# Six modulations computed two at a time, and their two gates spread through DRAM

## The reference, cut to what matters

```python
def adaln(cvec, w, b):                       # w: 1024 x 6144, b: 6144
    m = jax.nn.silu(cvec) @ w + b
    return m.reshape(cvec.shape[0], N_MOD, D_MODEL)

def modulate(h, m, i):
    return h * (1.0 + m[:, i + 1][:, None, :]) + m[:, i][:, None, :]

h = modulate(rmsnorm(x, norm1_g), m, 0)      # m[0], m[1]
x = x + m[:, 2][:, None, :] * mixer(h)       # m[2], a gate
h = modulate(rmsnorm(x, norm2_g), m, 3)      # m[3], m[4]
x = x + m[:, 5][:, None, :] * moe(h)         # m[5], a gate
```

## Time and profile before

| | |
|---|---|
| timed executions | 899.17, 900.0, 901.62 us |
| profiled execution, own time | 896.39 us |
| its span, first to last instruction | 894.5 us |
| TensorE busy | 855.6 us (96%) |
| VectorE busy | 491.5 us (55%) |
| ScalarE busy | 242.8 us (27%) |
| GpSimd busy | 87.0 us (10%) |
| read from HBM | 279.82 MB |

### The profile page before, as it was taken

The page is one execution under the profiler, slowest core; times in us unless marked ns, Lnnn a source line. Parts: engine busy times, 40 slices in busy tenths (PEclk is TensorE's granted clock), DMA queues, the critical chain, the costliest instruction groups (busy, mean ns, idle before and its releaser), DMA issues.

```text
span 894.5 us, 13521 instructions
## 1 busy us (share of the span) xinstructions
PE 855.6 (96%) x4887; PEld 501.8 (56%) x4887; DVE 491.5 (55%) x1016; ACT 242.8 (27%) x398; POOL 87.0 (10%) x202
## 2 busy tenths in 40 slices
PE   3799999999999999999999999999999999999993
PEld 2387875899999874434444444444444444444441
DVE  1663384486667456245646464646464646464575
ACT  3537643444423241221111111121112121112122
POOL 8410000000001060000000000000000000000000
PEclk9999999999999999999999999999999999999997
DMA  9974877622225377499999999999999999999931
GB/s 353 343 288 163 299 290 255 141 95 95 95 95 170 149 296 317 190 413 409 416 420 403 410 420 419 404 416 419 420 421 414 420 421 421 417 420 404 421 126 70
DMA packets 76596, 280.82 MB, mean 314 GB/s; under 512 B 14340, under 2 KB 30784, under 8 KB 51584
## 3 DMA queue, kind: packets, MB, share of 16 engines
q1 hardware_dynamic: 61488, 260.06, 73.3%
q0 software_dynamic: 6352, 15.52, 4.6%
q10 hardware_dynamic: 8704, 4.54, 2.0%
HBM read 279.82 MB, written 5.51 MB: 319 GB/s over the span
## 4 chain that ended last, share of the span: by engine, by line
PE 90%; DMA 5%; DVE 3%; issue 1%; ACT 0%; ACTq 0%; DVEq 0%
PE bank L1488 26%; PE bank L1507 13%; PE bank L1516 11%; PE bank L1090 8%; PE bank L1092 7%; PE bank L1091 7%; PE bank L1476 4%; DMA chunk_raw<-in_w_ada_dram 3%; PE bank L1360 2%; DMA b_t<-in_b_ada_dram 2%; PE bank L1600 2%; PE bank L1118 1%; PE bank L1170 1%; PE bank L1404 1%; PE bank L1203 1%; PE bank L1277 1%
## 5 line engine op out<-in xcount | busy, mean ns | idle before, releaser
L1488 PE MATMUL bank<-gu,x_t 128*32 128x512 f32 (+2 forms) x1408 | 240.6, 594 | 0.0
L1488 PEld LDWEIGHTS bank<-gu,x_t 128*32 128x32 f32 (+2 forms) x1408 | 75.6, 124 | 147.4 <-issue 146.7
L2125 DVE TENSOR_TENSOR ffn_acc<-ffn_acc,bank 128x512 f32<-128x512 f32 x192 | 120.4, 683 | 7.8 <-PE bank L1516 6.6
L1507 PE MATMUL bank<-dn,a_t 128*32 128x512 f32 (+2 forms) x704 | 123.9, 596 | 0.0
L1050 ACT ACTIVATE silu_sb<-bank 128x256 f32<-128x256 f32 x34 | 13.0, 384 | 320.8 <-PE bank L1488 320.8
L2067 DVE TENSOR_TENSOR act_sb<-silu_sb,bank 128x256 f32<-128x256 f32 x34 | 14.3, 421 | 149.9 <-ACT silu_sb L1050 149.9
L1090 PE MATMUL bank<-h_hi,chunk_lo 128*128 128x384 f32 x240 | 84.2, 351 | 0.0
L2117 DVE SCALAR_TENSOR_TENSOR y_lo<-bank,slot_gate,y_hi 128x512 fp32r<-128x512 f32 x68 | 50.9, 748 | 55.8 <-ACT y_hi L1040 55.5
L1092 PE MATMUL bank<-h_hi,chunk_hi 128*128 128x384 f32 x240 | 80.6, 336 | 0.0
L1091 PE MATMUL bank<-h_lo,chunk_hi 128*128 128x384 f32 x240 | 80.4, 335 | 0.0
L747 POOL DMA_INDIRECT xg<-h_dram,slot_tok x34 | 33.9, 997 | 456.5 <-DVE slot_tok L1941 456.2
(11 more groups left out here) (359 smaller groups left out, 1043.2 us busy)
## 6 DMA issues: line engine op xcount, KB each, us to landing
gu<-in_w_gate_e_dram SPq DMA_DIRECT2D x64, 1024.0 KB, 10.3
gu<-in_w_up_e_dram SPq DMA_DIRECT2D x64, 1024.0 KB, 13.6
dn<-in_w_down_e_dram SPq DMA_DIRECT2D x64, 1024.0 KB, 14.2
chunk_raw<-in_w_ada_dram SPq DMA_DIRECT2D x24, 1024.0 KB, 8.5
chunk_raw<-in_w_in_dram SPq DMA_DIRECT2D x18, 1024.0 KB, 5.5
chunk_raw<-in_w_out_dram SPq DMA_DIRECT2D x4, 1024.0 KB, 5.1
chunk_raw<-in_w_pa_dram SPq DMA_DIRECT2D x2, 1024.0 KB, 5.0
chunk_raw<-in_w_pb_dram SPq DMA_DIRECT2D x2, 1024.0 KB, 5.0
```

The lines of the kernel that those rows point to most:

```text
L1488: mm = pe.matmul(bank[2 + u % 2][at_x, :].rearrange("p (g n) -> p g n", g=2), x_t[:, cols], wide[:, :, k, :], start=(k == 0), stop=(k == K ...
L1507: mm = pe.matmul(outs[half][at_x, :], a_t[:, cols], dn[slot_of(x, first)][:, wc], start=(k == 0), stop=(k == 1))
L2125: dve.tensor_tensor(ffn_acc[t][:, cols], ffn_acc[t][:, cols], out[:, :], ALU.add).then_inc(S["place_out"], 1)
```

## The change

- `w_ada` is now read one `k` slice a chunk, for two modulations at once: (0, 1), (3, 4) and (2, 5), eight chunks a pair. The four column groups hold two modulations by two halves, and the eight chunks accumulate in one bank. No partial sums are left over.
- For the pairs (0, 1) and (3, 4) the half is not a run of 512 columns, but columns `n * 8 + k` for four values of `k`: the moving operand is read with a stride of 8 elements. Then four plain 128-column transposes turn the bank, and VectorE needs one addition (with the bias) per modulation.
- The pair (2, 5), both gates, uses bank 7 with plain runs. VectorE adds the bias (`bias_rows`, loaded earlier) and halves the rows of gate 2, and the attention's first scores wait for it. POOL stores the rows to DRAM (`gate_dram`) and loads them back to all partitions, `gate_mix` at once and `gate_ffn` when the projections are over. `pick`, `m_late` and the eight spreading matmuls with their copies are gone.
- The first projection waits for `h_t` piece by piece, at first for one piece of ScalarE and two of VectorE.

```diff
-                if kind == "ada" and i < 8:
...
+                if kind == "ada":
+                    m, k = MODS[2 * (i // KD):2 * (i // KD) + 2], i % KD
+                    sp.dma_start(dst[:, :].rearrange("p (m n) -> p m n", m=2),
+                                 w_ada[0].rearrange("(p k) (m n) -> p k m n", k=KD, n=D)[:, k, m[0]:m[1] + 1:m[1] - m[0], :]).then_inc(loaded, 16)
...
-            pool.tensor_copy(m_late[:, :], m_row[1][:, :]).then_inc(S["late_row"], 1)
+            pool.wait_ge(S["ada_row"], NMOD)
+            for c in range(2):
+                pool.dma_start(gate_dram[c:c + 1, :].rearrange("a (q n) -> (a q) n", q=NQ), gate_rows[c:P:QW, :]).then_inc(S["gate_stored"], 16)
+            pool.wait_ge(S["gate_stored"], 32)
+            pool.wait_ge(S["gates_mm"], 16)
+
+            def spread_rows(dst, n, loaded):
+                pool.dma_start(dst[:, :, :], gate_dram[:, D * n:D * n + D].unsqueeze(0).to_broadcast([P, 2, D])).then_inc(loaded, 16)
+
+            spread_rows(gate_mix, 0, S["mix_loaded"])
             pool.wait_ge(S["w_mm"], NPROJ)
+            spread_rows(gate_ffn, 1, S["ffn_gate_loaded"])
...
-            spread_copy(0, gate_mix, 0.5)
...
+            def modulate(i):
+
+                n, (m, k) = number[("ada", i)], divmod(i, KD)
+                pe.wait_ge(chunk_loaded[slot[n]], arrival[n])
...
+                for q in range(NQ):
+                    cols = chunk_raw[slot[n]][:, q // 2 * D:q // 2 * D + D]
+                    if m < 2:
+                        mm = pe.matmul(bank[6][q * QW:(q + 1) * QW, :].rearrange("p (k n) -> p k n", k=4), cond_t[:, k, :],
+                                       cols.rearrange("p (n k) -> p k n", k=KD)[:, 4 * (q % 2):4 * (q % 2) + 4, :],
+                                       start=(k == 0), stop=(k == KD - 1))
+                    else:
+                        mm = pe.matmul(bank[7][q * QW:(q + 1) * QW, :], cond_t[:, k, :],
+                                       cols[:, 512 * (q % 2):512 * (q % 2) + 512], start=(k == 0), stop=(k == KD - 1))
+                mm.then_inc(S["ada_mm"], 1)
+
+            def turn_rows(m):
+                pe.wait_ge(S["ada_row"], m + 1)
+                for j in range(4):
+                    mm = pe.transpose(bank[6][:, j * P:(j + 1) * P], m_row[m][:, j * P:(j + 1) * P], ident[:, :])
                 mm.then_inc(S["m_spread"], 1)
...
-                        if n == 0 and k % 4 == 0:
-                            pe.wait_ge(S["h_ctx"], k // 4 + 1)
-                            pe.wait_ge(S["h_made"], k // 4 + 1)
+                        if n == 0:
+                            pe.wait_ge(S["h_ctx"], k + 1)
+                            pe.wait_ge(S["h_made"], max(k + 1, 2))
...
-                spread(n, bank[4 + n % 2], m_row[0])
-            pe.wait_ge(S["ada_row"], NADA // 2)
+            later(7)
+            pe.wait_ge(S["ada_row"], NMOD)
...
+            def modulations(m):
+
+                dve.wait_ge(S["m_spread"], m + 1)
+                by_half = bank[6][:, :].rearrange("p (j a h c) -> p a h j c", j=4, a=2, h=2)
+                for a in range(2):
+                    i = MODS[2 * m + a]
+                    dve.tensor_tensor(mod_t[:, i, :, :].rearrange("p (h j) c -> p h j c", h=2), by_half[:, a, :, :, 0:2],
+                                      b_t[:, i, :].rearrange("p (h j) -> p h j", h=2).unsqueeze(3).to_broadcast([P, 2, 4, 2]),
+                                      ALU.add).then_inc(S["mod_copied"], 1)
+
+            def gates_in_rows():
+                dve.wait_ge(S["ada_mm"], NADA)
+                dve.wait_ge(S["row_biased"], 64)
+                go(dve.tensor_tensor(gate_rows[:, :], bank[7][:, :], bias_rows[:, :], ALU.add))
+                dve.tensor_scalar(gate_rows[0:HALF, :], gate_rows[0:HALF, :], 0.5, None, ALU.mult).then_inc(S["ada_row"], 1)
```

More of the change, by code:

```diff
@@ L189, in hybrid_step @@
         ob_hi = at("ob_hi", [P, CT, NTOK], EX + 111.25, F32R)
-        m_late = at("m_late", [P, D], 28)
-        m_row = [at(f"m_row{i}", [P, D], EX + 155.5 + 4 * i) for i in range(2)]
+        m_row = [at(f"m_row{i}", [P, 512], EX + 155.5 + 2 * i) for i in range(2)]
+        gate_rows = at("gate_rows", [P, 512], EX + 159.5)
+        bias_rows = at("bias_rows", [P, 512], EX + 161.5)
         block_w = at("block_w", [P, 2, 2, CT, P], 12)
@@ L791, in _ @@
             act.activation(cond_t[:, :, 0:2].rearrange("p k c -> p c k"), cond_raw[:, :, :], ACT.Silu).then_inc(S["cond_silu"], 1)
-            for a in range(2):
-                act.wait_ge(S["ada_mm"], 4 * a + 4)
-                act.activation(m_row[a % 2][:, 512:1024], bank[7][:, :], ACT.Copy).then_inc(S["ada_row"], 1)
             act.wait_ge(S["scale1_ready"], 1)
@@ L853, in grow @@
                                    bias=by[:, t:t + 1]).then_inc(S["e2_done" if dst is gate_e else "a_done"], 1)
-            def spread_copy(i, dst, scale):
-                for n in range(4):
-                    act.wait_ge(S["bc_mm"], 8 if i and n == 2 else 4 * i + n + 1)
-                    act.activation(dst[:, n // 2, 512 * (n % 2):512 * (n % 2) + 512], (spread_bank(n) if i else bank[4 + n % 2])[:, :],
-                                   ACT.Copy, scale=scale).then_inc(S["bc_evac"], 1)
             for n in range(4):
@@ L1122, in turn_rows @@
-            def turn_rows(a):
-                pe.wait_ge(S["ada_row"], 2 * a + 2)
-                for k in range(KD):
-                    mm = pe.transpose(bank[6 + k // 4][:, (k % 4) * P:(k % 4 + 1) * P], m_row[a % 2][:, k:D:KD], ident[:, :])
-                mm.then_inc(S["m_spread"], 1)
-            def spread(n, out, row):
-                pe.matmul(out[:, :], pick[:, n // 2, :], row[:, 512 * (n % 2):512 * (n % 2) + 512],
-                          start=True, stop=True).then_inc(S["bc_mm"], 1)
@@ L1132, in modulate_first @@
-            def modulate_first(a):
-                for c in range(4):
-                    n = number[("ada", 4 * a + c)]
-                    pe.wait_ge(chunk_loaded[slot[n]], arrival[n])
-                    if n == 0:
-                        pe.wait_ge(S["cond_silu"], 1)
-                    if c == 0 and a:
-                        pe.wait_ge(S["mod_copied"], a)
-                    for h in range(2):
-                        for j in range(2):
-                            q = 2 * ((c + h) % 2) + j
-                            at_w = j * D + 512 * h
-                            mm = pe.matmul(bank[6 + h][q * QW:(q + 1) * QW, :], cond_t[:, 2 * c + j, :],
-                                           chunk_raw[slot[n]][:, at_w:at_w + 512], start=(c < 2), stop=(c >= 2))
-                    mm.then_inc(S["ada_mm"], 1)
@@ L1665, in _ @@
             dve.wait_ge(S["cond_loaded"], 80)
-            for a in range(2):
-                dve.wait_ge(S["ada_mm"], 4 * a + 4)
-                row(a, 0)
-                mod_sum(a)
+            dve.wait_ge(S["ada_mm"], KD)
+            dve.tensor_copy(m_row[0][:, :], bank[6][:, :]).then_inc(S["ada_row"], 1)
+            modulations(0)
             dve.wait_ge(S["mod_copied"], 2)
@@ L1712, in _ @@
             low(3)
-            row(2, 0)
             low(4)
```

161 lines of the change are left out of this document (48 added, 113 removed).

## The result

| | before | after |
|---|---|---|
| median of the timed runs, us | 899.17 (898.86 to 901.62, 5 runs) | 905.61 (903.84 to 907.53, 5 runs) |
| ratio of the two, with its 95% interval | | 1.0066 (1.0045 to 1.0086) |
| profiled execution: span, granted clock | 894.5 us, 0.991 | 903.8 us, 0.986 |

The changed kernel is slower by 0.66%. The forecast was 889.8 us, in a range of 886.5 to 901.5: wrong, and on the wrong side. The medians are 6.4 us apart and the two profiled spans 9.3, because the profiled execution of before (896.39 us) was one of its faster ones; so some 2.9 us of what the traces differ by need not be the change's. A race of that size, which one profile wins and the other loses, is told under e6 and e9.

A forecast was written before the change was run, and what follows sets the result against it. TensorE, with 90% of the chain of waits, was taken as the bound. Savings of 2.2 + 1.3 + 0.5 + 2.35 + 3.9, say 10.2 us, taken from 900.0 gave 889.8 us, range 886.5 to 901.5.

The forecast's parts named there:

- Columns taken eight apart: Modulation matmuls of 16 of 24 chunks: reading the moving operand at stride 8 was taken to cost nothing, factor 1.
- the nearest row: Transposes of m_row: a weight load at the same stride, 189 ns against 140 contiguous, used to choose factor 1.
- The transfers at the start: First sixteen w_ada chunks: 8 KB runs in place of 4 KB were to save 0.5 us, at most 0.7.
- The ladder: TensorE and VectorE steps from the eighth chunk to the first projection: 1.7 us saved, 2.2 with the transfers.
- its three items: Start: four fewer transposes 0.44 us, VectorE additions about 0.2, waiting for two h_t pieces instead of four 0.93.
- Transposes and waits among the projections: Among the projections: fewer transposes save 1.3 us; waits for w_ada chunks, between 0 and 1.3, taken as 0.5.
- The spread before the attention: Between last modulation and first scores: dropping four spreading matmuls was to gain 2.35 us, between 2.0 and 2.6.
- The cover behind it: First attention step: a 4.4 us projection was to hide row maxima starting 2.2 us behind the scores; failure 0.5 us.
- The trip through DRAM: Gates stored and reloaded on POOL's queue, 1 MB per gate: costed at nothing, 2.5 us if a late transfer were hit.
- The spread in the first expert block: Between blocks 0 and 1 of the expert loop: dropping the second gate's spread was to gain 3.9 us.
- The rival that happened: Strided modulation matmuls take twice as long, 3.4 us at the start and 7.4 among projections: 901.1 us, chance 0.12.

The follow-up runs named there:

- e6: Changed kernel with SyncE's next 2 MB expert load held until GpSimd has issued the first gather of expert rows: 906.26 us, ratio 1.0084.
- e9: Changed kernel with SyncE's next 2 MB expert load held until the first gather of expert rows has landed: 902.51 us, ratio 1.0041.
- e1: Only fp32 matmuls on resting data, contiguous or strided, no full kernel: a set of four groups takes 0.86 us contiguous, 1.84 at stride 8.
- e4: Changed kernel with modulation matmuls reading contiguous halves, columns reordered afterwards by sixteen small matmuls in place of four transposes: 901.89 us, ratio 1.003.
- e3: Changed kernel with the paired chunks of modulations 0, 1 and 3, 4 read in 4 KB pieces again, not 8 KB: 898.94 us, ratio 1.0006.
- e2: Changed kernel with a separate semaphore for cond_raw, so the Silu no longer waits for g1, g2 and b_t: 899.27 us, ratio 1.0007.
- e10: Changed kernel with the edits of e2, e4, e5 and e9 together: 889.43 us, ratio 0.9888.
- e5: Changed kernel with the first gate's 1 MB spread (gate_mix) issued only after both attention bias tables have landed: 904.18 us, ratio 1.0056.
- e8: Kernel before with the one edit of e6, the expert load held behind the first gather's issue: 898.86 us, ratio 0.9993.
- e11: Kernel of e10 with the last two chunks of the gates' modulations moved ahead of the last projection: 892.72 us, ratio 0.9948.

## Why the prediction was wrong, point by point

- **Columns taken eight apart: the step that failed.** The text took a factor of 1, "the value of the nearest row"; it is 2 (1.86 us a chunk against 0.93; e1, e4). That is 3.2 us at the start (first chunk to end of the eighth: 14.90 against 11.67) and 7.8 among the projections, where the sum had nothing. The row was a weight load. That the transposes behind it follow each other quickly says nothing of the moving operand, and the row's own number, 189 against 140 ns, already said that the stride is not free. The sentence of the Trainium skill (SBUF — State Buffer, Door 1: The DMA port swizzle) on 16-byte lines that want two hits agrees with e1: stride 2 is nearly free (0.90 us), stride 4 and 8 pay. Its other figure, that fp32 may be strided by 4 for nothing, is not what e1 measured (1.82 against 0.86 us). I gave the case 0.12, and named its sign, the matmuls of one chunk well over 1.07 us. Alone it led to the 901.1 us of the rival; the next point is what went beyond.
- **The transfers at the start: the second step that failed.** Forecast as 0.5 us won by longer pieces. The six chunks issued first land by 23.6 us in before, 23.4 in after, 23.5 with 4 KB pieces (e3) and 22.9 in e9, so 0.1 to 0.6 was there, while the same longer pieces made `b_t` 6 us later. The trace of before had it: TensorE's wait of 1.86 us for `cond_t` stands in the earlier trace rows, and the chain, of which the prediction used the shares by engine, begins with the 14.87 us of `b_t`. The modulations start 6.0 us later (23.94 against 17.97); with the 3.2 of the strides and 1.7 given back by the ladder that is the 7.5 us at the start. Either of e2 and e3 takes 6.4 to 7.6 us off it. With the Silu early the transfers are the bound there again, and the strides cost little: the first projection starts at 34.49 us in e2 and at 34.22 in e10.
- **The ladder.** From the end of the last modulation matmul to the first projection it is 3.2 us (38.84 to 42.05); in before it was 4.9 (29.64 to 34.56). The 1.7 forecast are there (its three items add up to 1.6); they are only paid out behind a later start. From the transposes to `h_t` it is 0.9 less, forecast 0.64, and from `h_t` to the projection 0.9 less, forecast 0.93.
- **Transposes and waits among the projections.** Forecast 1.3 + 0.5. The stretch to the scores grew by 2.2; strided pairs add 4 x 1.94 = 7.8, the spread takes off 2.4, so 3.2 are left for these two terms: 1.3 from the waits for chunks, which all went, and 1.9 from the transposes and what I cannot place (0.6).
- **The spread before the attention.** Forecast 2.35. Matmuls' end to scores: 152.90 to 156.55 before, 3.65; now 164.97 (163.05 and 1.92) to 166.24, 1.27. So 2.4 are won, with the wait of 1.3 for `gate_rows` that was foretold. The cover behind it held: the first row maxima start 2.07 us behind the scores (0.52 in before), and the first attention step takes 5.01 us as before.
- **The trip through DRAM "at nothing".** Wrong by 1.2 us. It is not late for anyone, but its 1 MB meets the bias tables' issue on ScalarE (e5). The text asked only whether the data would be late, and not whom the transfer holds up while it runs.
- **The spread in the first expert block.** Forecast 3.9, measured 3.9 between the two blocks, and the stream of weights keeps up. But 2.5 us were lost just ahead of it (0.8 and 1.7 in the table): a gather and a load that were 1.4 us apart in before's trace left together, and the gather took 4.3 us longer. The text has no term for this. By the trace of e5 it is not a sure cost of the change: the same code at this place, with the clock low elsewhere, does not lose it.
- **The rival that happened** was priced at 901.1 us. Its own parts hold: 3.2 at the start (priced at 3.4) and 7.8 among the projections (7.4). The rest up to 905.6 comes from `b_t`, the bias tables and the gather, none of which was in the text.

## What to carry to other kernels

Before a layout is changed so that the moving operand is strided, time one matmul in it: with fp32, strides of 4 and 8 halved its speed here whatever the number of streams, and pieces of 16 bytes were free. When the pieces of a large load change size, look up every small load that shares the rings with it, and give each consumer a semaphore that waits only for what it reads. A transfer that nobody needs soon is not free: place it where no other issue and no race with a needed load stands beside it, and hold a race by what has landed, not by whose turn it is.

## What the runs showed of the hardware

- fp32 moving operand of 512 columns, a set of four groups: 0.86 us contiguous, 0.90 at stride 2, 1.82 at stride 4, 1.84 at stride 8, 0.86 for runs of four in every eight; at stride 8 one group alone takes as long (1.84).
- A chunk at stride 8 took 1.86 us at a granted clock of 0.50 (after, 24 to 28 us) as at 1.00 (e2); a contiguous one 1.93 at 0.50 and 1.07 at 1.00 (e4).
- 768 pieces of 32 bytes landed after 14.4 to 14.9 us beside 4 KB pieces (before, e3, e8), after 20.4 to 22.9 beside 8 KB pieces (the other nine traces).
- Two table loads took ScalarE 2.99 to 3.24 us to issue alone and 4.44 to 6.30 with a broadcast of 1 MB issued 1.7 to 2.8 us ahead of them; 5.50 in after.
- A gather of 128 rows of 4 KB landed after 4.3 to 4.8 us with no weights issued within the first 1.3 us, and after 8.7 to 9.5 when 2 MB were issued up to 0.4 us behind it.
- Between the first projection and the expert loop all profiles but that of e11 have a stretch of 10 us with a granted clock of about 0.83 (0.66 in e2 and e3), often right behind a wait of TensorE of 1 us or more; 0.83 over 10 us is 1.7 us. Its place moved: 320 to 330 us in before, 370 to 380 (0.85) in after, 110 to 120 in e10, with no such wait near. All traces have the wait of 1.3 us at the second norm alike; before, e5, e6, e8 and e9 have the low clock behind it, the others not, and what decides it is open. Part of the difference of single stretches is this and not the edit.
